# Latent attention in a two-block transformer kernel: who makes the high and low parts of keys and queries

## The reference

```python
q = (rms_norm_2(c_q, cq_g) @ w_uq).reshape(b, s, MLA_HEADS, MLA_NOPE + MLA_ROPE)
kv = (rms_norm_2(c_kv, ckv_g) @ w_ukv).reshape(b, s, MLA_HEADS, MLA_NOPE + MLA_V)
...
q = rms_norm_2(q, q_g)
k = rms_norm_2(k, k_g)
... # rope on the last 32 features of both
scale = (MLA_NOPE + MLA_ROPE) ** -0.5
logits = jnp.einsum('bqhd,bkhd->bhqk', qb, k) * scale
logits = jnp.where(chunk_mask(q_pos, k_pos), logits, -jnp.inf)
p = jax.nn.softmax(logits, axis=-1)
return jnp.einsum('bhqk,bkhd->bqhd', p.astype(v.dtype), v)
```

## Time and profile before

| what | value |
|---|---|
| median of 3 executions | 3175.22 us (3173.71 to 3175.61) |
| profiled execution, its own time | 3174.81 us |
| its span | 3173.0 us |
| TensorE busy, share of the span | 3069.1 us, 97% |
| VectorE, ScalarE, GpSimd busy | 52%, 45%, 23% |
| mean granted TensorE clock | 0.989 of full speed |

### The profile page before, as it was taken

How to read it: one execution, slowest core, us unless ns; L and a number is a source line. 1 busy time by engine, 2 the same in 40 slices (tenths; PEclk the granted TensorE clock), 3 DMA queues, 4 the chain that set the end, 5 groups by cost and what they waited for, 6 DMA issues and landing times.

```text
span 3173.0 us, 43952 instructions
## 1 busy us (share of the span) xinstructions
PE 3069.1 (97%) x13727; PEld 2430.3 (77%) x13727; DVE 1644.8 (52%) x2441; ACT 1434.9 (45%) x2100; POOL 736.7 (23%) x508
## 2 busy tenths in 40 slices
PE   8999999999999999999999989999999988999998
PEld 6888888788887777888867767788887776778887
DVE  6544445575665977574657573511125756441113
ACT  4333333443333675343356764522345666542224
POOL 2333323100000000000023213244443220334444
PEclk9999999999999999999999999999999999999999
DMA  5333322333333232433222112133332220223334
GB/s 160 95 104 93 88 81 73 95 114 99 97 93 93 60 106 80 135 96 96 75 65 67 59 37 67 47 93 93 98 119 69 57 66 21 67 73 93 93 93 132
DMA packets 490394, 273.00 MB, mean 86 GB/s; under 512 B 9550, under 2 KB 479766, under 8 KB 489848
## 3 DMA queue, kind: packets, MB, share of 16 engines
q1 hardware_dynamic: 485576, 264.45, 29.0%
q10 hardware_dynamic: 4656, 6.58, 0.6%
HBM read 267.69 MB, written 12.21 MB: 88 GB/s over the span
## 4 chain that ended last, share of the span: by engine, by line
issue 56%; PE 30%; POOL 11%; DVE 2%; ACT 1%; POOLq 0%; ACTq 0%; DMA 0%; DVEq 0%
PE acc L753 9%; PE acc L754 9%; PE acc L759 8%; POOL s_w_lo L722 5%; POOL s_w_lo L721 5%; PE acc L756 1%; PE wide L785 1%; PE misc L754 0%; PE misc L753 0%; PE misc L759 0%; DVE s_sc L2610 0%; PE wide L753 0%; POOLq L111 0%; PE wide L754 0%; ACTq L1670 0%
## 5 line engine op out<-in xcount | busy, mean ns | idle before, releaser
L753 PE MATMUL acc<-s_h_hi,s_w_hi 128*128 128x512 f32 (+1 forms) x1920 | 787.8, 410 | 15.5 <-DVE s_h_lo L3053 9.2
L754 PE MATMUL acc<-s_h_lo,s_w_hi 128*128 128x512 f32 (+1 forms) x1920 | 753.2, 392 | 0.0
L721 POOL TENSOR_TENSOR s_w_lo<-s_raw,s_w_hi 128x512 fp32r<-128x512 f32 x212 | 274.9, 1297 | 2020.9 <-ACT s_w_hi L1623 2020.0
L759 PE MATMUL acc<-s_h_hi,s_w_lo 128*128 128x512 f32 (+1 forms) x1680 | 659.4, 393 | 0.0
L1623 ACT ACTIVATE s_w_hi<-s_raw 128x1024 fp32r<-128x1024 f32 x386 | 409.3, 1060 | 386.1 <-DVE s_x L3308 210.8
L753 PEld LDWEIGHTS acc<-s_h_hi,s_w_hi 128*128 128x128 f32 x1920 | 363.3, 189 | 115.6 <-issue 19.9
L754 PEld LDWEIGHTS acc<-s_h_lo,s_w_hi 128*128 128x128 f32 x1920 | 363.7, 189 | 87.5 <-issue 12.3
L759 PEld LDWEIGHTS acc<-s_h_hi,s_w_lo 128*128 128x128 f32 x1680 | 317.6, 189 | 73.1
L704 POOL TENSOR_TENSOR s_w_lo<-s_raw,s_w_hi 128x1024 fp32r<-128x1024 f32 x80 | 191.5, 2394 | 406.2 <-ACT s_w_hi L1623 404.6
L722 POOL TENSOR_TENSOR s_w_lo<-s_raw,s_w_hi 128x512 fp32r<-128x512 f32 x212 | 279.0, 1316 | 0.0
L753 PE MATMUL acc<-s_hid_hi,s_w_hi 128*128 128x512 f32 x704 | 278.1, 395 | 0.0
(11 more groups left out here) (498 smaller groups left out, 5416.4 us busy)
## 6 DMA issues: line engine op xcount, KB each, us to landing
s_raw<-w_ff SPq DMA_DIRECT2D x128, 512.0 KB, 4.0
s_raw<-ffn_w_up SPq DMA_DIRECT2D x96, 512.0 KB, 3.9
s_raw<-attn_w_qkv SPq DMA_DIRECT2D x72, 512.0 KB, 3.8
s_raw<-ffn_w_down SPq DMA_DIRECT2D x48, 512.0 KB, 4.0
s_raw<-w_in SPq DMA_DIRECT2D x48, 512.0 KB, 4.0
s_raw<-lru_w_in SPq DMA_DIRECT2D x16, 512.0 KB, 4.0
s_raw<-w_out SPq DMA_DIRECT2D x16, 512.0 KB, 4.0
s_bd<-bias_by_head SPq DMA_DIRECT2D x24, 256.0 KB, 5.0
```

The source lines that it names most:

```text
L721: pool.tensor_tensor(w_lo_b[s][:, 0:h, :], raw_b[s][:, 0:h, :], w_hi_b[s][:, 0:h, :].bitcast(F32), ALU.subtract)
L753: mm(out, ahi, bhi, start=start, stop=False, **kw)
L754: mm(out, ahi, blo, start=False, stop=False, **kw)
L759: mm(out, alo, bhi, start=False, stop=stop, **kw)
```

## The change

In the latent heads, VectorE makes the high parts of keys and queries itself, by a copy behind each product (`mla_scaled`), ScalarE makes none of them any more (`mla_root` holds only the Ln and Exp), and the low parts are made by GpSimd (`latent_los`), which stands in GpSimd's program behind the first 30 units of a layer. The factor 96^-0.5 on the queries goes into their 1/rms: the Ln is taken of the sum of squares plus 96 eps, in place of the mean plus eps, so that the copies need no factor. GpSimd's loop over groups of 4 units becomes a loop over layers with 104 units written out.

```diff
+            def latent_los():
+                for h in range(HEADS_2):
+                    for (hi, lo), src in ((mla_k[h % 2], kr[0:MLA_W, :]), (mla_q[h % 2], tn[0:MLA_W, 0, :])):
+                        pool.wait_ge(sems["mla_hi"], count("mla_hi"))
+                        pool.tensor_tensor(lo, src, hi.bitcast(F32), ALU.subtract).then_inc(sems["mla_lo"], 1)
+                        pool.wait_ge(sems["mla_lo"], count("mla_lo"))
+
+            before_latent = len(UNITS_2) + 4 + 2 + 2
+            with count.loop(LAYERS, "hi_split unit_ready mla_hi mla_lo"):
+                units_by_halves(before_latent)
+                latent_los()
+                units_by_halves(UNITS_LAYER - before_latent)
+            units_by_halves(AHEAD_2)
...
                 def mla_scores(h):
-                    pe.wait_ge(sems["hn_lo"], count("hn_lo", 2))
+                    pe.wait_ge(sems["mla_lo"], count("mla_lo", 2))
...
-                def mla_hi(h):
+                def mla_root(h):
...
                     fn(rs_k, rs_k, ACT.Exp, scale=-0.5).then_inc(sems["hn_rstd"], 1)
                     act.wait_ge(sems["hn_rstd"], count("hn_rstd"))
-                    freed()
-                    fn(mla_k[h % 2][0], kr[0:MLA_W, :], ACT.Copy).then_inc(sems["hn_hi"], 1)
-                    act.wait_ge(sems["hn_hi"], count("hn_hi"))
...
-                    freed()
-                    fn(mla_q[h % 2][0], tn[0:MLA_W, 0, :], ACT.Copy, scale=MLA_W ** -0.5).then_inc(sems["hn_hi"], 1)
-                    act.wait_ge(sems["hn_hi"], count("hn_hi"))
...
-                head_rstd(MLA_W, MLA_W)
-                mla_hi(0)
+                head_rstd(None, MLA_W)
+                mla_root(0)
+                act.wait_ge(sems["mla_hi"], count("mla_hi", 2))
                 square_output()
                 norm_output(SUB)
                 memory_values_hi()
                 for h in range(HEADS_2):
+                    if h:
+                        act.wait_ge(sems["mla_hi"], count("mla_hi", 2))
                     if h < HEADS_2 - 1:
                         mla_squares(h + 1)
-                        head_rstd(MLA_W, MLA_W)
+                        head_rstd(None, MLA_W)
...
-                def mla_lo(h):
+                def mla_scaled(h):
+                    if h:
+                        dve.wait_ge(sems["mla_lo"], count("mla_lo", 2))
                     dve.wait_ge(sems["hn_rstd"], count("hn_rstd", 2))
                     output()
                     tt(kr[R, :], tn[R, 1, :], rs_k[R, :], ALU.mult).then_inc(sems["acc_freed"], 1)
                     dve.wait_ge(sems["acc_freed"], count("acc_freed"))
+                    nc.vector.tensor_copy(mla_k[h % 2][0], kr[R, :]).then_inc(sems["mla_hi"], 1)
+                    count("mla_hi")
                     o = output()
                     tt(tn[R, 0, :], o[R, :], rs[R, :], ALU.mult).then_inc(sems["acc_freed"], 1)
                     dve.wait_ge(sems["acc_freed"], count("acc_freed"))
-                    head_lo(mla_k[h % 2][1], kr[R, :], mla_k[h % 2][0])
-                    head_lo(mla_q[h % 2][1], tn[R, 0, :], mla_q[h % 2][0], MLA_W ** -0.5)
+                    nc.vector.tensor_copy(mla_q[h % 2][0], tn[R, 0, :]).then_inc(sems["mla_hi"], 1)
+                    count("mla_hi")
```

More of the change, by code:

```diff
@@ L279, in build_program @@
             "hn_sq hn_rstd hn_norm hn_hi hn_lo om_full po_full po_freed a_mid rot_full "
-            "l_sum mla_norm mla_ln kr_in rope_done mla_sq l_abs l_done z_full a_exp sq32 ".split())
+            "l_sum mla_norm mla_ln mla_hi mla_lo kr_in rope_done mla_sq l_abs l_done z_full a_exp sq32 ".split())
         sems = {n: ctx.enter_context(nc.semaphore(n)) for n in names}
@@ L302, in build_program @@
         mask_r = sb("mask_r", [P, 2, P], F32R)
-        eps = sb("eps", [P, 1])
+        eps = sb("eps", [P, 2])
         raw = [sb(f"raw{n}", [P, KC, P]) for n in range(RING_A)]
@@ L727, in _, with units_by_halves @@
             count.second_ring()
-            with count.loop((LAYERS * UNITS_LAYER + AHEAD_2) // RING_B,
-                            "hi_split unit_ready") as i:
-                for _ in range(RING_B):
+            def units_by_halves(n):
+                for _ in range(n):
                     unit_by_halves()
+            def latent_los():
[10 more added lines that the diff above has]
+            units_by_halves(AHEAD_2)
         @block.tensor
@@ L1595, in _ @@
             with count.loop(LAYERS,
-                            "mla_sq acc_freed acc_full h_lo hid_lo hn_lo hn_sq m_lo misc_act misc_dve kr_in o_lo om_full "
+                            "mla_sq mla_lo acc_freed acc_full h_lo hid_lo hn_lo hn_sq m_lo misc_act misc_dve kr_in o_lo om_full "
                             "l_sum p_ready po_freed po_full rot_full ss_ready stat_full unit_ready v_turned wide_freed "
@@ L2031, in head_rstd @@
                     act.wait_ge(sems["hn_norm"], count("hn_norm", 0))
-                    fn(dst, misc[0:rows, 0:n], ACT.Ln, bias=eps[0:rows, 0:1], scale=1.0 / features).then_inc(sems["misc_act"], 1)
+                    fn(dst, misc[0:rows, 0:n], ACT.Ln, bias=eps[0:rows, 0:1] if features else eps[0:rows, 1:2],
+                       scale=1.0 / features if features else 1.0).then_inc(sems["misc_act"], 1)
                     act.wait_ge(sems["misc_act"], count("misc_act"))
@@ L2298, in layer @@
                     if h < HEADS_2 - 1:
-                        mla_hi(h + 1)
+                        mla_root(h + 1)
                     else:
@@ L2405, in _ @@
             with count.loop(LAYERS,
-                            "mla_sq a_exp acc_freed acc_full exp_done h_hi hi_split hid_hi hid_lo hn_hi hn_norm hn_rstd "
+                            "mla_sq mla_hi a_exp acc_freed acc_full exp_done h_hi hi_split hid_hi hid_lo hn_hi hn_norm hn_rstd "
                             "hn_sq kr_in l_abs l_done m_hi misc_act mla_ln mn_in nmax_ready o_hi om_full po_freed pt_hi raw_B0 "
@@ L2469, in _ @@
             dve.wait_ge(sems["zeroed"], count("zeroed"))
-            nc.vector.memset(eps[:], EPS).then_inc(sems["zeroed"], 1)
+            nc.vector.memset(eps[:, 0:1], EPS)
+            nc.vector.memset(eps[:, 1:2], MLA_W * EPS).then_inc(sems["zeroed"], 1)
             dve.wait_ge(sems["zeroed"], count("zeroed"))
@@ L3170, in layer @@
                 mla_values()
-                mla_lo(0)
+                mla_scaled(0)
                 head_norm([(yo[:, 5, :], od[:], 0)], "sb_out_g_2")
@@ L3192, in layer @@
                     if h < HEADS_2 - 1:
-                        mla_lo(h + 1)
+                        mla_scaled(h + 1)
                     else:
@@ L3197, in layer @@
                         turned_a(q)
+                count("mla_lo", 2)
                 ys(range(3, 7))
@@ L3317, in _ @@
             with count.loop(LAYERS,
-                            "mla_sq a_mid acc_freed acc_full bd_cut bd_in exp_done h_hi h_lo hid_hi hid_lo hn_hi hn_lo hn_norm "
+                            "mla_sq mla_hi mla_lo a_mid acc_freed acc_full bd_cut bd_in exp_done h_hi h_lo hid_hi hid_lo hn_hi hn_lo hn_norm "
                             "hn_rstd kr_in l_done l_sum m_hi m_lo misc_dve mla_norm mn_in nmax_ready o_hi o_lo "
```

## The result

The changed kernel takes 3179.02 us (median of 15 runs, 3177.4 to 3185.22), the kernel before 3174.89 in its 15 runs of the same batch: a ratio of 1.0017, 95% interval 1.0010 to 1.0024. That is 4.1 us, a small loss: the median lies within the 0.2% that the prediction called no change, and the interval reaches a little past it. The profiled execution took 3180.93 us, against 3174.81 before.

A forecast was written before the change was run, and what follows sets the result against it. TensorE, busy 3069 of 3173 us; in the latent heads VectorE bounds K to S, TensorE and ScalarE S to K. Per layer 0.67 + 3 x 0.64 - 2 x 0.04 = 2.51; two layers add 5.0 to 3174.81: 3179.8 us, range 3175.0 to 3184.0.

The forecast's parts named there:

- Relief won almost nothing: VectorE and ScalarE do less work; from S to K this wins 0.04 us for heads 1 and 2 of each layer.
- The step from S to K: From start of a head's scores to start of the next scaled keys; bound by TensorE and ScalarE, staying 8.9 to 9.0.
- K to S + 0.64: From start of scaled keys (K) to start of next head's scores (S): 3.69 us becomes 4.33, for three heads.
- The estimate of 1.35 us: GpSimd's subtraction by the skill's ratio of 1.96, in place of 1.29; the result would be some 0.8 us later.
- The second copy is held: VectorE's copy of the queries waits on GpSimd's subtraction of the keys, ending twice 0.15 us behind it, at K + 2.91.
- the rival without it: Second copy not held, S at K + 4.00: loses 0.31 us a head, 0.20 in head 0; 3176.9 us; chance 0.17.
- Head 0 + 0.67: ScalarE's square in head 0 waits for both VectorE copies, so all four heads of the layer shift by 0.67 us.
- Behind head 3, nothing: TensorE's idle time before head 3 grows from 3.04 to 3.7 us; the clock's fall stays in place; nothing counted.
- The clock ahead of heads 1 and 2 stays high: TensorE's idle time there becomes 1.27 us, under the 2.24 that once passed without a fall, so no fall.
- The rival that had 0.05: Clock falls ahead of heads 1 and 2: four slow stretches, up to 3.4 us each, 13.6 in all, 3193; chance 0.05.
- Sum: Per layer 0.67 + 3 x 0.64 - 2 x 0.04 = 2.51 us; two layers 5.0, giving 3179.8 us.

The follow-up runs named there:

- Experiment 3: Changed kernel with the low parts of keys and queries made by VectorE in place of GpSimd: 3176.00 us, ratio 1.0006.
- experiment 4: Changed kernel with the sum of the next head's squares ahead of the scores in TensorE's order: 3169.79 us, ratio 0.9983.
- Experiment 2: Changed kernel with the queries' high part copied by ScalarE again: 3176.70 us, ratio 1.0010.
- experiment 1: Changed kernel with head 0's square on ScalarE ahead of the wait for VectorE's two copies: 3181.42 us, ratio 1.0021.
- experiment 10: experiment 1 plus four unread matmuls on TensorE ahead of the wait for GpSimd in heads 1 and 2: 3179.59 us, ratio 1.0016.
- 5: Kernel before the change, with the sum of squares moved ahead of the scores on TensorE: 3187.48 us, ratio 1.0037.
- 6: Changed kernel with the edits of experiment 1 and experiment 4 together: 3168.09 us, ratio 0.9982.
- 9: Kernel of experiment 8 with the low parts made by VectorE in place of GpSimd: 3165.66 us, ratio 0.9974.
- 7: Changed kernel with 14 unread matmuls on TensorE ahead of head 3's wait for GpSimd: 3177.23 us, ratio 1.0010.
- experiment 8: Changed kernel with sum ahead of scores, head 0's square ahead of its wait, and 14 unread matmuls before head 3: 3165.15 us, ratio 0.9971.

## Why the prediction was right, point by point

The forecast of 3179.8 is 0.8 above the median, and its mechanism is the one that the profile shows. Its steps:

- **Relief won almost nothing: right.** The step from S to K is 8.86, 8.89 and 8.96 us after in the first layer, 8.86, 8.99 and 8.98 before. I gave it 0.04 twice a layer; it is 0.12 in the first layer and 0.03 in the second. Experiment 3 confirms it with GpSimd taken out, and experiment 4 shows why: TensorE's order held the next root back, and once the sum stood ahead of the scores, up to 2.2 us a head were won.
- **K to S + 0.64: the mechanism right, the size 0.58.** GpSimd's subtractions took 1.29 and 1.26, one at the row's median and one at its minimum. VectorE's first copy started at K + 0.72, not 0.82, and GpSimd's second subtraction ended at K + 4.14, not 4.28; TensorE started 0.13 behind it instead of 0.05, which leaves 0.06. The estimate of 1.35 us, made beside the forecast from a ratio of 1.96, would have been too long (the Trainium skill has that ratio in "GPSIMD Engine Reference", section "Elementwise — side-by-side cycle accounting", not in the section named).
- **The second copy is held: right.** It ends 0.27 behind GpSimd's first subtraction (taken: 0.30) and takes 874 to 1028 ns in all 8 of its executions. Experiment 2 prices the hold at 0.21 us a head in K to S (4.06; the rival without it had 4.00). Its time of 3176.7 against the rival's 3176.9 proves nothing, as its slow clock differs. By the Trainium skill, "SBUF — State Buffer", section "Who interferes with whom", a VectorE copy in a two-port mode and a GpSimd instruction lock each other out for a whole instruction; the trace agrees, 1.01 us against 0.42.
- **Head 0 + 0.67: right in size** (0.66 and 0.64), by the step that I named, since moving the square took it away (experiment 1).
- **Behind head 3, nothing: wrong in detail.** From S of head 3 to the first weight unit the first layer gained 0.68 us. I had said that the fall stays where it is and more slow time passes idle; instead the fall came later, 1.0 us behind the start of the scores, so that the first of them ran at 2.4 GHz. In the second layer 1.5 us of slow time did pass idle, but the stretch lasted 10.2 us instead of 6.8, and the layer lost 0.18. The sum over both is 0.50 less than counted.
- **The clock ahead of heads 1 and 2 stays high: nearly.** The lengthened idle times of 1.20 and 1.22 us passed without a fall, as predicted. But in the first layer the clock fell some 2 us behind another idle time, of 1.47 us, that the kernel before has as well (1.46) and passes at full clock; the products of head 2 ran slower, and K to S of head 1 is 4.45 us instead of 4.27. And I had held 1.27 us of idle time safe because 2.24 had passed once without a fall. Experiment 1 shows that this argument does not hold: the same 1.2 us of idle time was followed by a fall there and not in the changed kernel. The rival that had 0.05 was closer than I gave it, in its condition; its price per fall, up to 3.4 us, was too high: 2.4 in experiment 1.
- **Sum.** By layer: 0.66 + 1.78 - 0.68 = 1.76 and 0.64 + 1.72 + 0.18 = 2.54, 4.30 together, where the prediction had 2.51 and 2.51. The errors in K to S and behind head 3 make the loss smaller than forecast, head 1 of the first layer makes it 0.17 larger, and the profiled run's extra 1.8 us lies outside. That the sum came so near is in part luck: each layer has 3.4 us more of slow clock than before, which the forecast left out, and in this arrangement it cost next to nothing; in experiment 2, with 6.8 more, the step behind head 3 is 1.1 and 1.2 us longer than before.

**What stays open.** Why the clock fell in experiment 1 and not in the changed kernel, since the wait ahead of head 2 is equal, is not settled; experiment 10 shows only that work placed there moves the fall away. The stage accounts for the medians to within 1.2 us in the changed kernel and experiments 1, 3, 4, 5, 6, 9 and 10, less well in experiments 2, 7 and 8: its sum over both layers, against before's, is +4.9, -0.1 and -10.9 us there, and the medians +2.5, +2.9 and -9.2. A profile shows one execution, and the executions of one kernel can lie 9 us apart (experiment 4); the one profiled there, at 3173.48, has 3.6 us more outside the stage than before's.

## What to carry to other kernels

Before work is moved off an engine, read which engine bounds each step of the chain: here VectorE bounded one step and TensorE's own order the next, so the relief of ScalarE was worth nothing until the sum that the next head waits for stood ahead of the scores, which turned a loss of 4 us into a gain of 4, and of 9 with the square and the filling matmuls. A move to GpSimd costs twice on a chain: its own longer instruction (1.29 us against 0.69), and the VectorE copy that starts beside it (1.01 against 0.42); a copy on ScalarE or a subtraction that reads PSUM in that place is not held. In a kernel where TensorE is busy 97% of the time, add up the slow-clock time per stage of each version, for it lay between nothing (experiment 8, second layer) and 20.5 us a layer (experiment 5).

## What the runs showed of the hardware

- An idle time of 1.2 us ahead of the scores of head 2 (1.21 and 1.20) was followed by a fall of the granted clock from 2.4 to 1.2 GHz in experiment 1, in both layers, and by none in the changed kernel. In experiment 8 an idle time of 2.73 us behind head 3 was followed by a fall in the first layer, and one of 2.72 in the second by none. The length of one idle stretch did not tell a fall here.
- The copy that GpSimd holds ends about 0.27 us behind GpSimd's instruction, where a free one takes 0.42: by these figures most of its work comes after the hold.
- Two subtractions on VectorE that don't wait for each other started 0.61 us apart, less than their 0.69 each. Where each waited for the one ahead, it was 0.82 before; the changed kernel's first copy, which waits for the product ahead of it, starts 0.72 behind that product.
- GpSimd's subtraction takes as long with 96 partitions as with 128: 1.26 to 1.30 us, where the median of the weight units is 1.29.
